# Two weight sums of a Strassen-Winograd block pair made by accumulating transfers on GpSimd's queue, with the first blocks of a pair split two pairs ahead

## What is computed

```
def swiglu(h, w_in, w_out):
    gu = h @ w_in
    gate, up = gu[..., :D_FF], gu[..., D_FF:]      # D_FF = 2816
    return (jax.nn.silu(gate) * up) @ w_out
...
for i in range(DEPTH):
    f = swiglu(rms_norm(h, norm_pre[i, 0]), w_ffn_in[i, 0], w_ffn_out[i, 0])
    h = h + FFN_RES_WEIGHT * rms_norm(f, norm_post[i, 0])
    ...mixer...
    f = swiglu(rms_norm(h, norm_pre[i, 2]), w_ffn_in[i, 1], w_ffn_out[i, 1])
    h = h + FFN_RES_WEIGHT * rms_norm(f, norm_post[i, 2])
```

## Time and profile before

| | |
|---|---|
| median of 3 runs | 1763.61 us (1762.8 to 1764.61) |
| the profiled execution's own time | 1765.51 us |
| its span in the trace | 1763.7 us |
| PE busy | 1751.2 us, 99% |
| DVE busy | 1330.7 us, 75% |
| ACT busy | 832.4 us, 47% |
| POOL busy | 31.2 us, 2% |
| DMA, mean | 104 GB/s, 183.22 MB |

### The profile page before, as it was taken

One profiled execution on the slowest core, in us unless ns is written; L12 is line 12 of the kernel. 1 busy time (PEld: TensorE's weight loads), 2 busy tenths in 40 slices (PEclk: granted clock), 3 DMA queues, 4 the chain that ended last, 5 costly groups with the idle time before them and its releaser, 6 DMA issues.

```text
span 1763.7 us, 31054 instructions
## 1 busy us (share of the span) xinstructions
PE 1751.2 (99%) x12753; PEld 1571.5 (89%) x12753; DVE 1330.7 (75%) x1918; ACT 832.4 (47%) x1389; POOL 31.2 (2%) x63
## 2 busy tenths in 40 slices
PE   9999999999999999999999999999999999999999
PEld 7899899887588899899988998999887988998998
DVE  6899488589758897497588974966887788974964
ACT  5446255355835455255354552553424554552652
POOL 0000000032000000000000000000000000000000
PEclk9999999999999999999999999999998999999999
DMA  6333223322032333223223332332454223322331
GB/s 203 108 131 109 96 98 115 123 67 81 2 108 69 115 116 108 96 99 118 96 72 119 109 107 96 108 119 85 123 167 126 97 75 116 119 97 96 110 107 49
DMA packets 74438, 183.22 MB, mean 104 GB/s; under 512 B 23712, under 2 KB 30512, under 8 KB 74304
## 3 DMA queue, kind: packets, MB, share of 16 engines
q1 hardware_dynamic: 72128, 179.02, 30.7%
q0 software_dynamic: 1600, 1.52, 0.3%
q10 hardware_dynamic: 576, 0.79, 0.1%
HBM read 174.35 MB, written 6.29 MB: 102 GB/s over the span
## 4 chain that ended last, share of the span: by engine, by line
PE 97%; DVE 1%; DMA 1%; issue 0%; ACT 0%; SPq 0%; ACTq 0%; DVEq 0%
PE bank L866 36%; PE bank L525 16%; PE bank L526 16%; PE bank L527 16%; PE bank L618 4%; PE bank L623 2%; PE bank L927 1%; PE bank L959 1%; PE bank L1025 1%; PE bank L903 1%; PE bank L552 1%; PE bank L544 1%; PE bank L942 1%; PE bank L922 0%; PE bank L592 0%
## 5 line engine op out<-in xcount | busy, mean ns | idle before, releaser
L525 PE MATMUL bank<-a_hi,w_hi 128*128 128x512 f32 (+1 forms) x912 | 334.8, 367 | 1.1 <-issue 1.1
L526 PE MATMUL bank<-a_lo,w_hi 128*128 128x512 f32 (+1 forms) x912 | 332.9, 365 | 0.0
L527 PE MATMUL bank<-a_hi,w_lo 128*128 128x512 f32 (+1 forms) x912 | 332.7, 365 | 0.0
L1170 ACT ACTIVATE w_hi<-w_raw 128x1024 fp32r<-128x1024 f32 x192 | 202.7, 1058 | 198.4 <-DVE w_raw L1550 160.1
L866 PE MATMUL bank<-x_hi,w_hi 128*128 128x256 f32 x1024 | 290.1, 283 | 0.0
L866 PE MATMUL bank<-x_lo,w_hi 128*128 128x256 f32 x1024 | 289.7, 283 | 0.0
L866 PE MATMUL bank<-x_hi,w_lo 128*128 128x256 f32 x1024 | 289.6, 283 | 0.0
L1542 DVE TENSOR_TENSOR w_lo<-w_raw,w_hi 128x1024 fp32r<-128x1024 f32 x192 | 234.5, 1222 | 27.3 <-ACT w_hi L1170 26.4
L1530 DVE TENSOR_TENSOR w_lo<-w_raw,w_hi 128x1024 fp32r<-128x1024 f32 x142 | 173.6, 1223 | 90.7 <-ACT w_hi L1119 90.3
L1119 ACT ACTIVATE w_hi<-w_raw 128x1024 fp32r<-128x1024 f32 x142 | 146.6, 1052 | 198.1 <-PE bank L527 185.4
L866 PE MATMUL bank<-raw_forms_hi,w_lo 128*128 128x256 f32 x768 | 215.8, 281 | 0.0
(11 more groups left out here) (245 smaller groups left out, 2919.6 us busy)
## 6 DMA issues: line engine op xcount, KB each, us to landing
w_raw<-stream SPq DMA_DIRECT2D x312, 512.0 KB, 3.2
h_resid<-xT SPq DMA_DIRECT2D x8, 256.0 KB, 6.2
qT<-stream SPq DMA_DIRECT2D x8, 256.0 KB, 6.2
u_scratch<-V SPq DMA_DIRECT2D x8, 256.0 KB, 2.4
a_lo<-u_scratch SPq DMA_DIRECT2D x8, 256.0 KB, 3.0
qT<-z_scratch SPq DMA_DIRECT2D x8, 256.0 KB, 4.4
outT<-h_resid SPq DMA_DIRECT2D x10, 128.0 KB, 1.8
z_scratch<-kT SPq DMA_DIRECT2D x2, 256.0 KB, 4.6
```

The costliest lines, as they stand in the source:

```text
L525: nc.tensor.matmul(out, lw[0], lx[0], start=first, stop=False)
L526: nc.tensor.matmul(out, lw[0], lx[1], start=False, stop=False)
L527: return nc.tensor.matmul(out, lw[1], lx[0], start=False, stop=last)
L1170: nc.scalar.activation(units_to(w_hi, pair, split), units_from(pair, split), ACT.Copy).then_inc(s_uhi, 1)
```

## The change

Two of the sums are now made by transfers issued by GpSimd that add what they load to what stands in `raw`: block 2 is loaded again and added to block 1 (`s_t3`), then, once split 0 of the pair is done (`s_ulo0`), block 1 is loaded again as it stands in DRAM and added to block 0 (`s_t1`). The signs of forms and sums are turned so that only additions are needed there: L1550 goes, `third_sum` becomes 0+2, block 3 becomes `third_sum`+3, and the first form's `negative` variant and scale go. Split 0 has its own semaphores, and beyond the second pair it is made two pairs ahead, in the middle of the iteration. GpSimd issues all of a block's transfers in one loop (`added_blocks`).

```
-SPLITS = 4
+SPLITS = 3
...
-                    sp.wait_ge(s_ulo, SPLITS * pair + (4 if second else 2))
+                    sp.wait_ge(s_ulo, SPLITS * pair + (3 if second else 1))
...
+            def added_blocks(index):
+                for pair in range(first_pair(index, 1), first_pair(index + 1, 1)):
+                    at = FAST_AT[pair]
+                    pool.wait_ge(s_raw[at % RING], 16 * (at // RING))
+                    pool.dma_start(raw_block(pair, 1), stream[at + 1, :, 0:UNIT], accum_op=ALU.add
+                                   ).then_inc(s_t3[pair % 2], 16)
+                    pool.wait_ge(s_ulo0, pair + 1)
+                    pool.dma_start(raw_block(pair, 0), stream[at, :, UNIT:2 * UNIT], accum_op=ALU.add
+                                   ).then_inc(s_t1[pair % 2], 16)
...
             def units_hi(pair, split):
-                if split:
-                    act.wait_ge(s_usum, 3 * pair + split)
+                if split == 1:
+                    act.wait_ge(s_t1[pair % 2], 16 * (pair // 2 + 1))
+                    act.wait_ge(s_t3[pair % 2], 16 * (pair // 2 + 1))
+                if split > 1:
+                    act.wait_ge(s_usum, 2 * pair + split - 1)
...
                 for i in range(FAST):      # ACT
-                    if more_pairs:
+                    if i == 0:
                         pair_loaded(ahead)
-                        if i:
-                            act.wait_ge(s_up, multiplied(pair - 1, UP2))
-                        else:
-                            act.wait_ge(s_mm, n0 - 1)
+                        act.wait_ge(s_mm, n0 - 1)
                         units_hi(ahead, 0)
...
                         units_hi(ahead, 2)
                     else:
                         down_hi(n0 + 1, 1, pair - 1, UP7)
+                    if i < FAST - 2:
+                        pair_loaded(ahead + 1)
+                        act.wait_ge(s_up, multiplied(pair, UP2))
+                        units_hi(ahead + 1, 0)
                     silu_first(pair)
...
             def unit_sums(pair):           # DVE
-                dve.wait_ge(s_ulo, SPLITS * pair + 1)
-                nc.vector.tensor_tensor(both[:, 0:2 * UNIT], both[:, UNIT:3 * UNIT], both[:, 0:2 * UNIT], ALU.subtract
+                dve.wait_ge(s_t1[pair % 2], 16 * (pair // 2 + 1))
+                nc.vector.tensor_tensor(third_sum[:, :], raw_block(pair, 0), raw_block(pair, 2), ALU.add
                                         ).then_inc(s_usum, 1)
-                dve.wait_ge(s_usum, 3 * pair + 1)
-                nc.vector.tensor_tensor(third_sum[:, :], raw_block(pair, 2), raw_block(pair, 0), ALU.subtract
+                dve.wait_ge(s_usum, 2 * pair + 1)
+                dve.wait_ge(s_ulo0, pair + 1)
+                nc.vector.tensor_tensor(raw_block(pair, 3), third_sum[:, :], raw_block(pair, 3), ALU.add
                                         ).then_inc(s_usum, 1)
...
                 for i in range(FAST):      # DVE
+                    if i == 0:
+                        units_lo(ahead, 0)
                     if more_pairs:
-                        units_lo(ahead, 0)
                         unit_sums(ahead)
                         units_lo(ahead, 1)
                     else:
                         down_lo(n0, 0)
                     first_gate(pair)
+                    if more_pairs:
+                        units_lo(ahead, 2)
+                    if i < FAST - 2:
+                        units_lo(ahead + 1, 0)
                     if i:
                         first_up(pair - 1)
-                    if more_pairs:
-                        units_lo(ahead, 2)
-                    if i:
                         product(pair - 1)
```

More of the change, by code:

```diff
@@ L312, in build_program @@
         s_usum = sem("weight_blocks_summed")
+        s_uhi0, s_ulo0 = sem("first_weight_forms_hi"), sem("first_weight_forms_lo")
+        s_t1 = [sem(f"first_weight_sum{i}") for i in range(2)]
+        s_t3 = [sem(f"third_weight_sum{i}") for i in range(2)]
         s_uhi, s_ulo = sem("weight_form_hi"), sem("weight_form_lo")
@@ L513, in _ @@
                                         ).then_inc(s_v, 1)
+            added_blocks(1)
+            added_blocks(2)
             pool.wait_ge(s_mm, PW1)
@@ L838, in products @@
                     pair = pair0 + i
-                    pe.wait_ge(s_ulo, SPLITS * pair + SPLIT_OF[product] + 1)
+                    if SPLIT_OF[product]:
+                        pe.wait_ge(s_ulo, SPLITS * pair + SPLIT_OF[product])
+                    else:
+                        pe.wait_ge(s_ulo0, pair + 1)
                     out = bank[{UP1: X_BANKS[pair % 2], UP6: X_BANKS[pair % 2], UP7: X_BANKS[pair % 2],
@@ L1166, in units_hi @@
             def units_hi(pair, split):
-                if split:
-                    act.wait_ge(s_usum, 3 * pair + split)
-                nc.scalar.activation(units_to(w_hi, pair, split), units_from(pair, split), ACT.Copy).then_inc(s_uhi, 1)
+                if split == 1:
[3 more added lines that the diff above has]
+                    act.wait_ge(s_usum, 2 * pair + split - 1)
+                nc.scalar.activation(units_to(w_hi, pair, split), units_from(pair, split), ACT.Copy
+                                     ).then_inc(s_uhi if split else s_uhi0, 1)
             def pair_loaded(pair):
@@ L1175, in pair_loaded, with form_hi @@
                     act.wait_ge(s_raw[at % RING], 16 * (at // RING))
-            def form_hi(index, product, half, tok, scale=1.0):
+            def form_hi(index, product, half, tok):
                 act.wait_ge(s_xn, KD * index + KD // 2 * (half + 1))
-                nc.scalar.activation(form(0, product), x_block_of(half, tok), ACT.Copy, scale=scale).then_inc(s_fhi, 1)
+                nc.scalar.activation(form(0, product), x_block_of(half, tok), ACT.Copy).then_inc(s_fhi, 1)
             def sum_forms(n0, index):
@@ L1539, in units_lo, with form_lo @@
             def units_lo(pair, split):
[L1541 removed]
+                if split:
+                    dve.wait_ge(s_uhi, SPLITS * pair + split)
+                else:
+                    dve.wait_ge(s_uhi0, pair + 1)
                 nc.vector.tensor_tensor(units_to(w_lo, pair, split), units_from(pair, split),
[L1543 removed]
+                                        units_to(w_hi, pair, split).bitcast(F32), ALU.subtract
+                                        ).then_inc(s_ulo if split else s_ulo0, 1)
             def unit_sums(pair):
[L1548 to L1550 removed]
+                dve.wait_ge(s_t1[pair % 2], 16 * (pair // 2 + 1))
+                nc.vector.tensor_tensor(third_sum[:, :], raw_block(pair, 0), raw_block(pair, 2), ALU.add
                                         ).then_inc(s_usum, 1)
[L1552 to L1556 removed]
+                dve.wait_ge(s_usum, 2 * pair + 1)
+                dve.wait_ge(s_ulo0, pair + 1)
+                nc.vector.tensor_tensor(raw_block(pair, 3), third_sum[:, :], raw_block(pair, 3), ALU.add
                                         ).then_inc(s_usum, 1)
             form_count = [0]
[L1561 removed]
+            def form_lo(product, half, tok):
                 form_count[0] += 1
@@ L1565, in form_lo @@
                 hi, of = form(0, product).bitcast(F32), x_block_of(half, tok)
[L1566 to L1571, removed]
+                nc.vector.tensor_tensor(form(1, product), of, hi, ALU.subtract).then_inc(s_flo, 1)
             def normalised_x(sub, k):
@@ L1791, in first_up @@
                     nc.vector.tensor_tensor(U[:, pair % 2, HALVES[0]], bank[Z_BANKS[pair % 2]][:, 0:T // 2],
-                                            seen[1][pair % 2], ALU.add).then_inc(s_up1, 1)
+                                            seen[1][pair % 2], ALU.subtract).then_inc(s_up1, 1)
                 def second_up(pair):
@@ L1797, in second_up @@
                     nc.vector.tensor_tensor(U[:, pair % 2, HALVES[1]], bank[Z_BANKS[pair % 2]][:, 0:T // 2],
-                                            seen[2][pair % 2], ALU.add).then_inc(s_up2, 1)
+                                            seen[2][pair % 2], ALU.subtract).then_inc(s_up2, 1)
                 def product(pair):
```

13 lines of the change are left out of this document (7 added, 6 removed).

## The result

The changed kernel takes 1833.86 us (median of 4 runs, 1831.2 to 1836.9) against 1763.74 us before: a ratio of 1.0398, 95% interval 1.038 to 1.0416, 70 us slower. The direction and the waits at stage starts had been forecast; waits from pair 2 on had not, and the size was three times the forecast, above the range.

What follows compares the result with a forecast made beforehand. PE was taken to bound the kernel, so DVE's saving was worth 0. At L = 3.6, waits of 3.2 and 2.2 us in four blocks gave 21.5 us: 1787.0 profiled, 1785 as median; range 1762 to 1822.

Steps and rivals of the forecast that it cites:

- What bounds the kernel: Pair stages: PE runs without a wait, 9.99 us a pair, so taking 78.3 us off DVE is worth 0.
- The wait at the stage start: PE waits at UP7 of pairs 0 and 1: 3.2 us in first stages, 2.2 in second, 21.5 us in all.
- L: Time from issue to landing of the adding transfer into block 0, put at 3.6 us.
- D: Delay of DVE's chain at a block's first stage, L - 2.56 where positive: 1.04 us at L = 3.6.
- The prediction's own formulas: First wait L + D - 2.15 in first stages, L - 2.14 in second; second wait L - 2.89 in both.
- From then on the cycle of DVE and GpSimd is 4.67 + L ... and no third wait comes: After the second wait of a stage, this cycle stays under PE's 9.99 us up to L = 5.3.
- keep their meaning: SP's queue: split 1 still frees the first slot, split 3 the second; a late split 1 delays the next load.
- near 0.5: DMA share in a stage with the adding transfers, up from 0.31 to 0.34: held to be no bound.
- The clock: Rival: PE's clock falls at the waits at stage starts, 7 us more, 1792 us; chance 0.15.
- Hidden: Rival: the accumulate lands within 2.55 us of issue, waits 0.4 us at most, taken as 1764 us; chance 0.11.
- Falling behind at every pair: Rival: from L = 5.3 on DVE and GpSimd set the pace; at 6.1 it costs 103 us, 1866; chance 0.16.
- The upper end of the range: 1822 us, for waits at stage starts only, L up to 5.2, with or without the clock.

Runs made afterwards that it cites:

- t3_only: Changed kernel with the adding transfer into block 0 removed and that sum made by DVE, the one into block 1 kept: 1764.42 us, 1.0005 against before.
- t3_later: Changed kernel with the adding transfer into block 1 held until the pair's second slot is loaded: 1810.29 us, 1.0266 against before.
- t1_only: Changed kernel with the sum into block 1 made by DVE, only the adding transfer into block 0 kept: 1825.54 us, 1.0347 against before.
- seen_first: Changed kernel; in a stage's first iteration ACT copies UP6 before waiting for transfers and DVE does first_gate before unit_sums: 1832.2 us, 1.038 against before.

## Why the prediction was wrong

**What bounds the kernel: right.** PE had no wait, DVE's work was wholly beside it, and t3_only, with 39 us of DVE work less, is the same as before.

**The wait at the stage start: right in place, L mis-sized.** The prediction's own formulas at L = 4.2: in first stages D = 1.64, waits 3.69 and 1.31; in second 2.06 and 1.31; four blocks 33.5 us. With L = 3.6 they gave 21.5; so 12 of the missing 49 us are this term. Measured at pairs 0 and 1: 27.3 + 7.3 = 34.6. That this comes so near is in part luck. The waits at pair 0 were longer than the formulas have them (4.0 to 4.7 and 2.3 to 2.5 us), GpSimd's late waking among the reasons; those at pair 1 were nearly nil in first stages (0 to 0.4) and 0.9 to 2.4 in second ones, where the t1 that counts landed in up to 6.1 us.

What sized L wrongly was to take the 512 KB load (3.2 us) as its price. An add of 256 KB took 4.2, and GpSimd's instruction 0.85 us, not 0.56. GpSimd also woke 0.30 us after DVE's end and not 0.05 (109.73 to 110.02 in the first stage, and never under 0.29 in the 64). The rule of the Trainium skill, "Collectives: The Full Stack" (Why ReduceScatter is half of AllGather), that two source reads halve the rate of an add, agrees with the queue rows: 11.9% of the engines' time for the adds, 5.9% for the same bytes as copies, with the 0.3% that the queue took before taken off. The latency worked out from it, 3.2 us, was a full microsecond short.

**"From then on the cycle of DVE and GpSimd is 4.67 + L ... and no third wait comes": the step that failed.** That cycle was near enough: with the slower waking 4.62 + 0.30 + 4.2 = 9.1 us, under 9.99, and t3_later and t1_only have no third wait. It was not the only one. The prediction let the waits on SP's queue "keep their meaning", because "the old order has a pair of lead"; but the new order puts split 0 two pairs ahead, which needs the second slot's load, in front of the split 3 that lets the next such load go. The loop that counts is load, split 0, split 3, next load, without t1 or the sums: 4.78 us and the load. At the 3.2 us of the loads before it would be 8.0. At the 5.0 to 7.1 us that the loads took here it was 11.6 us in the first stage (130.80 to 142.40), then 10.6 and 10.6. It cost 22.4 us. The step ahead of it, that a DMA share "near 0.5" is no bound, was right as an average (0.56 measured) and wrong as an argument: t1, t3 and a load are issued within some 2 us of each other. No run moved split 3 in front of that split 0, which would open the loop and leave both transfers; that rival remedy is untested.

**The clock: a rival, and it came on top.** 15.6 us of slow pace, where I had priced 7 and given it 0.15. The wait of 4.2 us brought a clock of 0.50 for 4.6 us; the one of 2.4 us in the second stage brought none, one as long in the fourth stage 2.0 us of slow pace. Most likely it also took up the wait at pair 1 in first stages, as the prediction said it would: 1.6 to 2.5 us were lost there ahead of it, against 1.31. No run shows this by itself.

**The other rivals.** Hidden: no; even a plain copy of 3.0 us is not hidden. Falling behind at every pair through L over 5.3: the effect is there, by another road. The upper end of the range: the prediction's formulas at L = 5.2 give 1817 us, and 1824 with its 7 us for the clock, not 1822, and at L = 2.8 they give 1770, not 1768; the measured time lies above either. Sum: 34.6 + 22.4 + 15.6 = 72.6, against 71.7 for the stages.

## What to carry to other kernels

Before moving work to a transfer, write down every loop of the new order, not only the one through the transfer, and price the loads in them beside the new transfers: t1 alone and t3 alone left this loop short enough, both together did not. A latency hidden by working two steps ahead is not hidden for the first steps of a stage; keep the old way there. And where PE waits is where the chain is late, not what makes it late: moving the waiting instruction only moved the wait.

## What the runs showed of the hardware

All of it is of this case's traces, in us from the start of the issuing instruction to landing.

An adding transfer of 256 KB on GpSimd's queue took 4.2 us (median of t1), a plain one 3.0, an adding one of 128 KB 3.2. The instruction took 0.85, 0.54 and 0.85 us, and often 1.18 where one was issued right behind another. GpSimd's instruction began 0.30 us (median of 64) after DVE's end released it.

Right behind another add, t3 took 5.1 to 5.8 us at stage starts, and 5.8 to 8.2 with a 512 KB load beside it. t1 with a load issued 0.5 to 0.6 us behind it took 5.6 to 6.1 us, 0.77 us behind 4.7 to 5.1, 0.87 us behind mostly 3.8 to 4.9 (t1_only, seen_first and the changed kernel among others). A second slot's plain load of 512 KB took 5.0 to 7.1 us beside both adds of the changed kernel in place of 3.1 to 4.2 before, and 3.1 to 6.0 in t3_only. How the DMA engines share themselves out no view here shows.

DVE's instructions kept their length beside GpSimd's issuing (L1577 in the changed kernel 693 ns, L1553 before 693).
